# Four slots of expert 0's weights fetched into the arena, with the token rows and the output sum in the residual buffers

## The reference

```python
N_EXPERTS = 16
CAPACITY_FACTOR = 2
D_FF_EXPERT = 2816
...
        x = x + jnp.einsum('bsc,cd->bsd', mixed, w_out)

        x = x + expert_choice_moe(rms_norm(x, norm2_g), w_router, w1, w3, w2)
```

## Time and profile before

| | us |
|---|---|
| median of 3 runs | 1902.13 |
| lowest and highest | 1900.67, 1903.8 |
| the profiled execution, its own time | 1906.49 |
| its span, first to last instruction | 1904.3 |
| DMA share of the chain that ended last | 50% |
| TensorE's share of that chain | 19% |
| DMA on SP's queue | 643.9 MB |
| TensorE's mean granted clock | 0.799 |

### The profile page before, as it was taken

The page is one execution under the profiler, slowest core; times in us unless marked ns, Lnnn a source line. Parts: engine busy times, 40 slices in busy tenths (PEclk is TensorE's granted clock), DMA queues, the critical chain, the costliest instruction groups (busy, mean ns, idle before and its releaser), DMA issues.

```text
span 1904.3 us, 23933 instructions
## 1 busy us (share of the span) xinstructions
PE 1425.0 (75%) x10492; PEld 830.6 (44%) x10492; DVE 273.5 (14%) x539; ACT 237.9 (12%) x529; POOL 37.0 (2%) x63
## 2 busy tenths in 40 slices
PE   5997899999999765866666675676757668476675
PEld 2674688888747332422323232232323323233232
DVE  1115200003972210000100001000010000101001
ACT  2223122002022200000000010000100001000010
POOL 0000000001110000000000000000000000000000
PEclk8998899999999677687767767767676676867767
DMA  9458234244251599999999999999999999999998
GB/s 353 148 201 343 110 136 176 94 172 153 89 220 68 227 424 432 432 439 424 439 425 438 427 436 430 433 433 429 437 427 437 426 428 435 438 425 439 423 441 343
DMA packets 47058, 648.94 MB, mean 341 GB/s; under 512 B 3800, under 2 KB 6304, under 8 KB 30000
## 3 DMA queue, kind: packets, MB, share of 16 engines
q1 hardware_dynamic: 43968, 643.90, 80.2%
q10 hardware_dynamic: 2848, 3.55, 0.5%
q0 software_dynamic: 208, 1.00, 0.1%
HBM read 647.38 MB, written 1.06 MB: 341 GB/s over the span
## 4 chain that ended last, share of the span: by engine, by line
DMA 50%; PE 19%; DVE 1%; issue 0%; ACT 0%; POOL 0%; SPq 0%; DVEq 0%; PEldq 0%; ACTq 0%; POOLq 0%
DMA ring<-in_w 50%; PE ps L1122 19%; DVE small L1020 0%; DVE arena L1070 0%; DVE arena L1072 0%; DVE arena L1016 0%; DVE arena L1114 0%; ACT L669 0%; ACT L657 0%; POOL arena L437 0%; SPq L359 0%; DVE arena L1089 0%; ACT arena L657 0%; PE ps L1617 0%; DVE arena L994 0%
## 5 line engine op out<-in xcount | busy, mean ns | idle before, releaser
L1122 PE MATMUL ps<-ring,arena 128*32 128x352 f32 (+2 forms) x6914 | 689.2, 556 | 393.6 <-DMA ring<-in_w 372.5
L1122 PEld LDWEIGHTS ps<-ring,arena 128*32 128x32 f32 (+1 forms) x6914 | 249.4, 134 | 715.8 <-issue 362.6
L1122 PEld LDWEIGHTS ps<-arena 128*128 128x128 f32 (+6 forms) x1044 | 168.2, 236 | 169.7 <-issue 139.6
L1122 PE MATMUL ps<-arena 128*128 (+10 forms) x1044 | 215.8, 377 | 29.5 <-DVE arena L1114 12.2
L1122 PE MATMUL ps<-hT,ring 128*128 128x256 f32 (+1 forms) x912 | 200.3, 382 | 6.8 <-ACT hT L591 3.5
L1122 PEld LDWEIGHTS ps<-hT,ring 128*128 128x128 f32 (+1 forms) x912 | 171.9, 189 | 35.3 <-issue 9.0
L1122 PE MATMUL ps<-arena,ring 128*128 128x256 f32 x768 | 173.0, 387 | 4.4 <-POOL arena L437 2.4
L1122 PEld LDWEIGHTS ps<-arena,ring 128*128 128x128 f32 x768 | 148.7, 195 | 27.4 <-issue 4.2
L701 ACT ACTIVATE arena<-ps,table 128x32 f32<-128x32 f32 x128 | 36.7, 287 | 447.8 <-PE ps L1122 447.8
L1114 DVE TENSOR_TENSOR arena<-arena,ps 128x512 f32<-128x512 f32 x64 | 41.7, 685 | 337.1 <-PE ps L1122 337.1
L1103 DVE TENSOR_TENSOR arena<-arena,ps 128x704 f32<-128x704 f32 x16 | 14.2, 888 | 525.0 <-ACT arena L705 525.0
(11 more groups left out here) (207 smaller groups left out, 443.8 us busy)
## 6 DMA issues: line engine op xcount, KB each, us to landing
ring<-in_w SPq DMA_DIRECT2D x77, 5632.0 KB, 32.5
ring<-in_w SPq DMA_DIRECT2D x19, 2816.0 KB, 30.7
ring<-in_w SPq DMA_DIRECT2D x35, 1408.0 KB, 32.7
ring<-in_w_ff SPq DMA_DIRECT2D x8, 4096.0 KB, 13.2
ring<-in_w_ada SPq DMA_DIRECT2D x6, 4096.0 KB, 14.0
ring<-in_w_in SPq DMA_DIRECT2D x4, 4096.0 KB, 17.6
ring<-in_w_out SPq DMA_DIRECT2D x2, 4096.0 KB, 13.9
ring<-in_w_in SPq DMA_DIRECT2D x3, 2048.0 KB, 10.8
```

Source lines behind the costliest of these rows:

```text
L1122: return pe.matmul(o, w, x, start=first, stop=last)
```

## The change

The stash: a new region of the arena, words 0 to 11,263, takes q12 to q15 of expert 0 (four slots), which before went to slots 0 to 3 of the ring once these were used. q12 to q14 are one DMA right behind q8; q15 waits for `std_set`, since its part of the arena holds the router's logits until then. Slots 0 to 3 of the ring, when expert 0 has used them, take expert 1's q0 to q3 in place of expert 0's q12 to q15, with the same waits. From there on every piece keeps its slot and its wait; only its place in the order of the queue is four chunks earlier in bytes.

To make room, `hnat` moves to `hT_`, `yacc` to `xT_`, `xe` to the front of `table`, `iota` to the front of `ada`, and the tiles of the routing and of the experts (`pick`, `he`, `sge`, `hTe`, `ye`, `pgs`, `pgT`, the routing's rows) move behind word 11,264. The arena grows by 136 words. TensorE's work for expert 0 is now written out ahead of the loop, since it reads the stash, and the loop covers experts 1 to 15. Five start-up semaphores become one.

```diff
+        stash = ar(0, 4 * SLOT)
+        yacc = xT_[:, :].rearrange("p (st n) -> p st n", st=ST)
+        hnat = hT_[:, :].rearrange("p (st n) -> p st n", st=ST)
+        pick = ar(11264, 1024, st=ST)
...
+        xe = table[:, 0:256].rearrange("p (c t) -> p c t", c=C)
...
             slots(0, 8, 1, piece_in[2])
-            for q, n, done in ((12, 1, s["refill_in"]), (13, 1, s["refill_in"]), (14, 2, piece_in[3])):
-                sp.wait_ge(s["w_used"], q + n - NSLOT)
-                slots(0, q, n, done)
-            for i, (q, n) in enumerate(PIECE_AT[4:]):
-                sp.wait_ge(s["w_used"], q + n - NSLOT)
-                piece(0, 4 + i)
-            with sp.Fori(0, NE - 1) as e:
+            stashed = mats[1][:, 0, (12 - C) * SLOT:]
+            sp.dma_start(stash[:, 0:3 * SLOT], stashed[:, 0:3 * SLOT]).then_inc(s["stash_in"], 16)
+            sp.wait_ge(s["std_set"], 1)
+            sp.dma_start(stash[:, 3 * SLOT:], stashed[:, 3 * SLOT:]).then_inc(piece_in[3], 16)
+            for q, n, done in ((0, 1, s["lead_in"]), (1, 1, s["lead_in"]), (2, 2, piece_in[0])):
+                sp.wait_ge(s["w_used"], q + n)
+                slots(1, q, n, done)
+            for i, (q, n) in enumerate(PIECE_AT):
+                if q > 12:
+                    sp.wait_ge(s["w_used"], q + n - NSLOT)
+                    piece(0, i)
+            for i, (q, n) in enumerate(PIECE_AT):
+                if q > 0:
+                    sp.wait_ge(s["w_used"], NCHUNK + q + n - NSLOT)
+                    piece(1, i)
+            with sp.Fori(0, NE - 2) as e:
                 for i, (q, n) in enumerate(PIECE_AT):
-                    sp.wait_ge(s["w_used"], NCHUNK * e + q + n + NCHUNK - NSLOT)
-                    piece(e + 1, i)
+                    sp.wait_ge(s["w_used"], NCHUNK * e + q + n + 2 * NCHUNK - NSLOT)
+                    piece(e + 2, i)
...
-                        if q in (4, 12):
-                            pe.wait_ge(s["first_in" if q == 4 else "refill_in"], 32)
                         w = ring[:, slot * SLOT:(slot + 1) * SLOT]
+                        if first and q >= 12:
+                            w = stash[:, (q - 12) * SLOT:(q - 11) * SLOT]
+                            pe.wait_ge(s["stash_in"], 16)
+                        elif first and q >= 4:
+                            pe.wait_ge(s["first_in"], 32)
+                        elif q == 0 and not first:
+                            pe.wait_ge(s["lead_in"], 32)
...
+            expert(0, first=True)
+            with pe.Fori(1, NE) as e:
+                expert(e)
```

More of the change, by code:

```diff
@@ L40 @@
 PIECES = (4, 4, 4, 4, 4, 2, 1, 1)
-AR = 14400
+AR = 14536
 UNITS = (["ada0", "ada1", "win_a", "win_b", "win_c", "win_d", "ada2", "ada3", "ada4", "ada5", "wout"]
@@ L218, in build @@
         one16 = ar(9736, 17)
-        iota = ar(9760, CAP)
+        iota = ada[:, 0:CAP]
         lgs = arena[0:17, 9800:9800 + S]
@@ L240, in build @@
         csq = ar(0, 1024, m=CT)
[L242 to L250, removed]
-        std, rst, nb = small[:, 72:74], small[:, 74:76], small[:, 76:78]
[L252 to L260, removed]
+        stash = ar(0, 4 * SLOT)
+        yacc = xT_[:, :].rearrange("p (st n) -> p st n", st=ST)
+        hnat = hT_[:, :].rearrange("p (st n) -> p st n", st=ST)
+        pick = ar(11264, 1024, st=ST)
+        restT, equalT, aboveT, countT, placeT = (arena[0:NE, 12288 + S * i:12288 + S * (i + 1)] for i in range(5))
+        he = ar(12288, 704)
+        sge = ar(12992, 704)
+        hTe = ar(12992, 704, r=FR)
+        ye = ar(13696, 256)
+        pgs = ar(13952, 256, st=ST)
+        pgT = ar(14208, 256)
+        aff = ar(14464, 32, st=ST)
+        rmx = ar(14496, 2)
+        rsm = ar(14498, 2)
+        top32 = arena[0:NE, 14500:14532]
+        ties = restT[:, 0:CAP]
+        room = arena[0:NE, 14532:14533]
+        std, rst, nb = small[:, 72:74], small[:, 74:76], small[:, 76:78]
+        xe = table[:, 0:256].rearrange("p (c t) -> p c t", c=C)
         filled = [sem(f"bank_filled{b}") for b in range(8)]
@@ L267, in build @@
         s = {name: sem(name) for name in """
-            small_in unit_used w_used ones_set eps_set pool_link scan_set qb1z_set e_set attz_set attd_set
+            small_in unit_used w_used const_set e_set attz_set attd_set
             att_set hid_used consts2_in upz_set conv_set cm_set acc_set gg2_set u2_set den_set epsd_set r1_set xr_set rsq_set qc_set cmean_set crec_set
@@ L273, in build @@
             sq1_set n1_set t1_set h_set relu_set x1_set sq2_set n3_set n2_set up_set sgb_set pe_link
-            qsq_set qk_set rs16_set v_set tmax_set texp_set uT_set csq_set diag_set cvar_set x2_set sq3_set first_in refill_in sqp_set
+            qsq_set qk_set rs16_set v_set tmax_set texp_set uT_set csq_set diag_set cvar_set x2_set sq3_set first_in stash_in lead_in sqp_set
             lge_set wr2_set std_set rst_set nb_set lgs_set hnat_set yinit_set xe_set ye_set xe_full sc_full pgT_set h1_full he_set sg_set
@@ L383, in _ @@
+            with sp.Fori(0, NE - 2) as e:
                 for i, (q, n) in enumerate(PIECE_AT):
-                    sp.wait_ge(s["w_used"], NCHUNK * e + q + n + NCHUNK - NSLOT)
-                    piece(e + 1, i)
+                    sp.wait_ge(s["w_used"], NCHUNK * e + q + n + 2 * NCHUNK - NSLOT)
+                    piece(e + 2, i)
         @block.gpsimd
         def _(pool):
-            nc.gpsimd.memset(ones[:, :], 1.0).then_inc(s["ones_set"], 1)
-            nc.gpsimd.memset(eps, EPS).then_inc(s["eps_set"], 1)
@@ L392, in _ @@
[L392 to L395, removed]
+            nc.gpsimd.memset(ones[:, :], 1.0).then_inc(s["const_set"], 1)
+            nc.gpsimd.memset(eps, EPS).then_inc(s["const_set"], 1)
+            nc.gpsimd.memset(scanm, 1.0).then_inc(s["const_set"], 1)
@@ L396, in _ @@
+            pool.wait_ge(s["const_set"], 3)
+            nc.gpsimd.memset(scanm.rearrange("p (n t) -> p n t", t=CH)[:, :, 0:1], 0.0).then_inc(s["const_set"], 1)
+            nc.gpsimd.memset(qb1, 0.0).then_inc(s["const_set"], 1)
             pool.wait_ge(s["e_set"], 4)
@@ L466, in _ @@
             act.sem_inc(s["small_in"], 16)
-            act.wait_ge(s["eps_set"], 1)
+            act.wait_ge(s["const_set"], 2)
             act.wait_ge(s["small_in"], 16 * 8)
@@ L766, in _ @@
             link(V.scalar_tensor_tensor(zz, zz, 0.0, tt, ALU.min, ALU.subtract))
-            dve.wait_ge(s["scan_set"], 1)
+            dve.wait_ge(s["const_set"], 4)
             link(V.tensor_tensor_scan(bb, scanm, zz, 0.0, ALU.mult, ALU.add))
@@ L780, in _ @@
             V.tensor_tensor(kl, kl, gk, ALU.mult).then_inc(s["gla_set"], 1)
-            dve.wait_ge(s["qb1z_set"], 1)
+            dve.wait_ge(s["const_set"], 5)
             V.scalar_tensor_tensor(qb1[CH:P, :], qb[CH:P, :], GDK ** -0.5, gq[CH:P, :], ALU.mult, ALU.mult)\
@@ L1141, in norm_sum @@
                 inc_filled(ins, label)
-            pe.wait_ge(s["ones_set"], 1)
+            pe.wait_ge(s["const_set"], 1)
             norm_sum("n_in", sq0, s["sq0_set"])
@@ L1577, in _, with expert @@
             pe.sem_inc(s["sc_full"], 1)
-            with pe.Fori(0, NE) as e:
+            def expert(e, first=False):
                 def gather(c):
```

## The result

The changed kernel takes 1890.69 us (median of 5 runs, 1889.2 to 1894.33), the kernel before 1902.53 (median of 5, 1900.67 to 1907.56). The ratio is 0.9929, 95% interval 0.9915 to 0.9943: some 13.5 us faster, 10.8 to 16.2 by the interval (the two medians alone are 11.8 us apart). The forecast was 1888.8 in 1886 to 1893.

A forecast was written before the change was run, and what follows sets the result against it. The prediction took weight bytes at 430 GB/s from 663 us as the bound: four chunks at 3.338 us leave the stream, all other terms 0, so 1902.13 - 13.35 = 1888.8 us, range 1886 to 1893.

The forecast's parts named there:

- The bound: From 663 us the weight queue is full at 430 GB/s; the end is the bytes left plus a 7.6 us tail.
- The stash fits: Four more chunks fill the empty queue at 628 to 640 us, ending about 641 us; routing slowed 0 to 0.5 us.
- The price: Four chunks fewer in the stream behind 662.77 us, at 3.338 us each: 13.35 us gained.
- The dry queue at 691 us: Queue empties at 691.2 us, expert 1's q4-q7 issued 687.98: 2.2 us spare, cost 0; rival: over 2 us, chance 0.07.
- the step about q23: Expert 0's last chunk is in by 691.2 us, so the first gathers end at 698.5 us instead of 700.64.
- Expert 1's q12 to q15: Issue needs `w_used` 28: four chunks end at 706.0 us at the higher clock, 712.5 at the lower; no loss.
- The cover to 717 us: Backlog of expert 1's q4 to q11 keeps the queue busy to 717.9 us: 11 us of cover, 4.5 at lower clock.
- The rival of code behind weights: TensorE's branch into the loop, about 697 us, waits for code behind weights; one wait up to 26.7 us; chance 0.04.
- the rule: Skill section: a taken branch to code not held must wait for a transfer; here at about 697 us, full queue.
- The range: Median time within 1886 to 1893 us, taking in the forecast and the dry-queue rival; faster by more than 0.2%: 0.93.

The follow-up runs named there:

- e3: Changed kernel with two chunks (q14, q15) in the stash instead of four; 1900.53 us, ratio 0.9963 to the kernel before.
- e6: Changed kernel with expert 1's q4 to q7 waiting for `w_used` 24 instead of 20; 1898.84 us, ratio 0.9950 to the kernel before.
- e2: Changed kernel without the stash: q12 to q15 go to ring slots 0 to 3 after use; 1905.89 us, ratio 0.9997 to the kernel before.
- e8: Kernel before, no stash, with 9 extra matmuls in TensorE's idle routing stretches; 1905.53 us, ratio 0.9994 to the kernel before.
- e1: Changed kernel with SP waiting for `w_used` 1 (about 640 us) before the stash's first transfer; 1898.38 us, ratio 0.9957 to the kernel before.
- e9: Kernel before, no stash, with 11 extra matmuls in TensorE's idle stretches; 1894.7 us, ratio 0.9942 to the kernel before.
- e5: Changed kernel itself, unaltered, measured again in a later series on another chip; 1894.16 us, ratio 0.9934 to the kernel before.
- e4: Changed kernel with expert 1's q2, q3 and expert 0's q16 to q19 issued one by one; 1889.0 us, ratio 0.9907 to the kernel before.
- e7: Changed kernel with 9 extra matmuls in TensorE's idle routing stretches; 1889.44 us, ratio 0.9913 to the kernel before.
- e11: Changed kernel with both the single-chunk issues and the 11 extra matmuls; 1883.92 us, ratio 0.9879 to the kernel before.
- e10: Changed kernel with 11 extra matmuls in TensorE's idle stretches; 1883.61 us, ratio 0.9883 to the kernel before.

## Why the prediction was right, step by step

**The bound.** Right: the time is the bytes left at 663 us, over 430 GB/s, and a tail. e3 and e6 show it from both sides, two chunks for 7.1 us and a queue left near empty for some 4 to 5 us for 3.1 to 4.7. The profiled executions bear it out over all versions. The rate from 614 to 664 us gives the bytes that have moved by then; what they are above the kernel before, over 430 GB/s, is what the span should lose:

| version | GB/s, 614 to 664 us | us less by these bytes | us less in span |
|---|---|---|---|
| before | 215 | 0 | 0 |
| e2, no stash | 213 | -0.2 | -0.9 |
| e8, nine matmuls, no stash | 217 | 0.2 | 1.7 |
| e3, half of the stash | 260 | 5.2 | 5.9 |
| e1, late stash | 280 | 7.6 | 8.0 |
| e9, eleven matmuls, no stash | 312 | 11.3 | 11.6 |
| changed | 318 | 12.0 | 12.1 |
| e5, changed again | 321 | 12.3 | 12.3 |
| e6, q4 to q7 late | 323 | 12.6 | 7.6 |
| e4, stash and single chunks | 369 | 17.9 | 17.4 |
| e7, stash and nine matmuls | 399 | 21.4 | 20.0 |
| e11, stash, single chunks, eleven matmuls | 409 | 22.6 | 22.8 |
| e10, stash and eleven matmuls | 416 | 23.4 | 24.0 |

All but e6 agree within 1.5 us. e6 falls 5.0 short, and it is the one version whose queue runs dry behind 664 us.

**The stash fits.** Right: 432 GB/s from 628 to 640 us, and at 649 to 651 the queue is empty again, so expert 1's q0 and q1 were in, as forecast. That the stash doesn't slow the routing or TensorE is borne out as well: `w_used` 8 was 0.45 us later, and 0.52 us of that existed at 616 us.

**The price.** 13.35 us was forecast; 13.5 and 12.6 were measured by ratio, 11.8 and 12.4 by medians, 12.1 in span. Where the gain comes from was put too simply, as four chunks moved into the hole; the number comes out either way. e1 shows that 8 of the 13 us are to be had with that hole left empty, since the two later ones serve as well, and e9 that the hole stays and 10 to 11 us are gained when TensorE frees the slots sooner. The hole is where the stash lands; what it buys is room ahead of `w_used` 8.

**The dry queue at 691 us.** The time was right, as e6 shows. The issue of q4 to q7 came at 686.61, 1.4 us earlier than the kernel before had it. There the step about q23 failed: I let it land by 691.2 us since the backlog ends then. TensorE after, beside the earlier trace rows:

```profile
686.98 2.37 PE L1131 MATMUL ps<-ring,arena 128*32 128x256 f32 x40 [0.43 <-DMA ring<-in_w]
690.37 1.50 PE L1131 MATMUL ps<-ring,arena 128*32 128x256 f32 x24 [1.02 <-DMA ring<-in_w]
693.75 1.50 PE L1131 MATMUL ps<-ring,arena 128*32 128x256 f32 x24 [1.89 <-DMA ring<-in_w]
...
697.76 1.72 PE L1131 MATMUL ps<-arena 32*128 32x256 f32 x8 [0.77 <-DVE xT L1123]
699.41 1.35 PE L1131 MATMUL ps<-arena,hT 128*128 x8
700.69 2.58 PE L1131 MATMUL ps<-ring,table 128*32 128x352 f32 x16
...
703.88 1.39 PE L1131 MATMUL ps<-ring,table 128*32 128x352 f32 x16
```

Its last passes start at 693.75, as they did before (693.35). My first reading was that q23 shares the engines with expert 1's q4 to q7, issued at 686.61. It doesn't hold: in e6, where these are issued at 695.15 only, TensorE gets q23 at the same time, with the queue near empty (23 GB/s) for nearly two us before:

```profile
693.59 1.50 PE L1131 MATMUL ps<-ring,arena 128*32 128x256 f32 x24 [1.86 <-DMA ring<-in_w]
```

So the last chunk can be used some 2 us behind the point at which the bulk of the bytes is out; what these 2 us are, no run separates. They don't seem to be the last chunk's alone: the passes on the chunk before it start 3.38 us earlier (690.37 us), which is about one chunk's price. The gathers thus ended at about 700.8 and not 698.5. q16 to q19 came in no earlier either (680.28 us, 679.91 before).

**Expert 1's q12 to q15.** Issued at 709.09; the forecast had 706.0 at the higher clock and 712.5 at the lower. The first chunk ran at the lower clock, 2.58 us at 700.69, and the next ones at the higher. The cover to 717 us was 8 us, not 11; nothing was lost.

**The rival of code behind weights.** Not seen. In the changed kernel three blocks of code moved between 700 and 760 us beside a full queue, where the kernel before moved none:

```profile
q1 hardware_dynamic: 933, 25.72, 99.7%
q8 instruction: 3, 0.05, 0.3%
```

and TensorE's rows above run on over the branch: scatter at 697.76, gathers at 699.41, first chunk at 700.69 us, with only 0.77 us of idle time named, for VectorE's sum ahead of the scatter's second half, and no other up to 715 us. The Trainium skill, "Runtime: NRT & Kernel Launch", section "Instruction fetch mechanics", says that a taken branch to code that isn't held stalls the engine. No such price is visible here. e2, which has the same branch, the moved tiles and no stash, measures 0.9997 (0.9988 to 1.0007), though its 6.78 us of waiting for weights could hide a shorter stall. Whether the target was held already at the branch no row tells, so the rule itself is neither borne out nor refuted.

**The range.** 1886 to 1893 held the median, 1890.69. In the series of e5 the changed kernel took 1894.16, outside it; the kernel before is itself 4.0 us slower there (1906.57 and 1902.53), and the ratios agree.

## What to carry to other kernels

If the end is set by a transfer queue, look for the stretches in which it is empty and ask what each waits for: more room, smaller pieces of the room there is, or a faster consumer. All three filled the same idle time here (13 us by room, then 4 to 5 by smaller pieces or about 10 by a faster consumer, which don't add up). Where an engine that frees the buffers has just idled, check its granted clock: eleven matmuls without use in a routing stage brought 10 to 11 us, nearly as much as four more buffers.

## What the runs showed that I hadn't expected

Two matmuls more or less went with the clock kept or lost. With nine, TensorE still sat idle 1.48 us ahead of the last routing transposes and 0.8 us ahead of the gathers, and the granted clock fell to 0.50: for 3.4 us in one profiled execution (e7), from 633.8 to 660.5 us in another (e8). e7's time scattered over 11.6 us between runs, where the kernel before on that chip scattered over 5.6. With eleven, the idle time was 0.62 us and nothing, the clock stayed at 1.00 from 628 to 659 us in the three profiled executions, and the runs of each version lie within 4.9 us. A chunk takes 1.88 us at the higher level and 3.50 at the lower. Why the same kernel keeps the clock in one run and not in the next stays open.
